# The low part of the FFN's gated tiles: subtracted by POOL instead of DVE

## The reference

```python
def swiglu(h, w_up, w_down):
    g, u = jnp.split(h @ w_up, 2, axis=-1)
    return (jax.nn.silu(g) * u) @ w_down
...
x = x + mix
x = x + swiglu(rmsnorm(x, norm_ffn[layer]), ffn_w_up[layer], ffn_w_down[layer])
```

## Time and profile before

| | us |
|---|---|
| median of 3 runs | 2603.36 |
| lowest and highest | 2598.88 and 2606.93 |
| the profiled execution's own time | 2599.3 |
| its span, first to last instruction | 2597.3 |

### The profile page before, as it was taken

How to read it: one execution, slowest core, us unless ns; L and a number is a source line. 1 busy time by engine, 2 the same in 40 slices (tenths; PEclk the granted TensorE clock), 3 DMA queues, 4 the chain that set the end, 5 groups by cost and what they waited for, 6 DMA issues and landing times.

```text
span 2597.3 us, 36699 instructions
## 1 busy us (share of the span) xinstructions
PE 2480.4 (95%) x15562; PEld 2217.9 (85%) x15562; DVE 1056.5 (41%) x1691; ACT 903.6 (35%) x1182; POOL 1266.8 (49%) x674
## 2 busy tenths in 40 slices
PE   7999998899999999999989899999978999999997
PEld 5889986688787888999979889988866779999997
DVE  3523245344335521544664451154475345222224
ACT  4332344342223412433444241344444223222222
POOL 5645454645545744533534474344342536544554
PEclk9999998999999999999989999999998999999999
DMA  4222233123232232222212222222222223222222
GB/s 161 90 79 73 74 124 102 62 77 110 90 105 81 92 97 97 74 82 82 90 49 90 74 92 94 93 90 73 86 74 96 84 98 122 90 90 91 88 90 82
DMA packets 72322, 233.17 MB, mean 90 GB/s; under 512 B 8768, under 2 KB 10848, under 8 KB 72160
## 3 DMA queue, kind: packets, MB, share of 16 engines
q1 hardware_dynamic: 72160, 230.82, 26.9%
HBM read 221.74 MB, written 9.05 MB: 89 GB/s over the span
## 4 chain that ended last, share of the span: by engine, by line
PE 80%; DVE 7%; ACT 3%; issue 3%; POOLq 2%; POOL 2%; DVEq 1%; DMA 1%; SPq 0%; ACTq 0%
PE ps L670 56%; PE ps L700 17%; POOLq L1172 2%; DMA wr<-in_wblk 1%; DVE xc L1682 1%; POOL wl L1166 1%; ACT wh L954 1%; DVE mixl L1508 1%; PE ps L759 1%; PE ps L757 1%; PE ps L763 1%; DVE sq L1315 1%; DVE vm L1705 0%; DVEq L1522 0%; POOL rsB L1178 0%
## 5 line engine op out<-in xcount | busy, mean ns | idle before, releaser
L1166 POOL TENSOR_TENSOR wl<-wr,wh 128x1024 fp32r<-128x1024 f32 (+2 forms) x396 | 950.6, 2411 | 619.9 <-ACT wh L954 619.1
L670 PE MATMUL ps<-xh,wh 128*128 128x260 f32 (+3 forms) x3312 | 896.5, 325 | 26.4 <-DVE xl L1328 14.8
L670 PE MATMUL ps<-xh,wl 128*128 128x260 f32 (+3 forms) x3312 | 881.7, 321 | 0.0
L670 PE MATMUL ps<-xl,wh 128*128 128x260 f32 (+3 forms) x3312 | 881.6, 321 | 0.0
L670 PEld LDWEIGHTS ps<-xh,wh 128*128 128x128 f32 (+1 forms) x3312 | 550.7, 189 | 90.8 <-issue 44.5
L670 PEld LDWEIGHTS ps<-xh,wl 128*128 128x128 f32 (+1 forms) x3312 | 549.3, 188 | 48.0 <-issue 2.0
L670 PEld LDWEIGHTS ps<-xl,wh 128*128 128x128 f32 (+1 forms) x3312 | 549.5, 189 | 45.7 <-issue 1.9
L954 ACT ACTIVATE wh<-wr 128x1024 fp32r<-128x1024 f32 (+2 forms) x396 | 409.5, 1044 | 481.7 <-DMA wr<-in_wblk 478.0
L700 PE MATMUL ps<-hidh,wh 128*128 128x260 f32 (+1 forms) x1056 | 289.4, 328 | 34.9 <-DVE hf L1529 13.5
L700 PE MATMUL ps<-hidl,wh 128*128 128x260 f32 (+1 forms) x1056 | 285.7, 325 | 0.0
L700 PE MATMUL ps<-hidh,wl 128*128 128x260 f32 (+1 forms) x1056 | 284.7, 324 | 0.0
(11 more groups left out here) (326 smaller groups left out, 2219.2 us busy)
## 6 DMA issues: line engine op xcount, KB each, us to landing
wr<-in_wblk SPq DMA_DIRECT2D x392, 512.0 KB, 3.7
xr<-in_xT SPq DMA_DIRECT2D x8, 260.0 KB, 5.8
xB<-in_xT SPq DMA_DIRECT2D x8, 260.0 KB, 4.5
out_yT<-xB SPq DMA_DIRECT2D x8, 260.0 KB, 2.2
xr<-in_xT SPq DMA_DIRECT2D x8, 256.0 KB, 5.8
xA<-in_xT SPq DMA_DIRECT2D x8, 256.0 KB, 4.3
Ss<-in_s_even SPq DMA_DIRECT2D x1, 2048.0 KB, 9.9
out_ss_even<-Ss SPq DMA_DIRECT2D x1, 2048.0 KB, 9.3
```

Source lines behind the costliest of these rows:

```text
L670: mm = pe.matmul(ps[0:cols, b + c, 0:n], wt[:, w], xt[:, e:e + n], start=first, stop=end)
L1166: pool.tensor_tensor(wl[n % 4][:, 0:w], wr[n % 4][:, 0:w], wh[n % 4][:, 0:w].bitcast(F32), ALU.subtract).then_inc(s_lo, 1)
```

## The change

`hidden_lo` is moved, word for word but for the engine, from DVE's block to POOL's, and the branch `hl` with it. The item's place in the list, its wait on `s_hh` (ACT's `hidh`) and its signal `s_hl` stay.

```diff
@@ POOL's block
+            def hidden_lo(L, X, g, k):
+                pool.wait_ge(s_hh, FI[L, X] * NF + 2 * g + k + 1)
+                t = slice((2 * (g % 2) + k) * W[X], (2 * (g % 2) + k + 1) * W[X])
+                pool.tensor_tensor(hidl[:, t], hf[:, t], hidh[:, t].bitcast(F32), ALU.subtract).then_inc(s_hl, 1)
...
+                elif k == "hl":
+                    hidden_lo(*v)
@@ DVE's block
-            def hidden_lo(L, X, g, k):
-                v.wait_ge(s_hh, FI[L, X] * NF + 2 * g + k + 1)
-                t = slice((2 * (g % 2) + k) * W[X], (2 * (g % 2) + k + 1) * W[X])
-                v.tensor_tensor(hidl[:, t], hf[:, t], hidh[:, t].bitcast(F32), ALU.subtract).then_inc(s_hl, 1)
...
-                elif k == "hl":
-                    hidden_lo(*z)
```

## The result

The changed kernel takes 2604.95 us (median of 21 runs, 2601.73 to 2606.66), the kernel before 2599.06 us (median of 21 runs, 2591.39 to 2606.93). The ratio, taken over all runs, is 1.0025, with a 95% interval of 1.0019 to 1.0032 (the two medians alone give 1.0023): some 6 us slower, where "no change" at 2603 us was forecast. The three runs that the forecast started from had a median of 2603.36 us, 4.3 us above that of all 21. So a time of 2605 us looked like no change against them and is a loss. One execution of 8591.87 us, in the kernel with six tiles taken back, is left out of its ratio.

A forecast was written before the change was run, and what follows sets the result against it. PE, busy 95% of the span, was taken to bound the kernel. Terms 0 + 0 - 3.0 + 0.5 + 1.6 + 0.6 = -0.3 us gave 2599.0, and with the runs' median 4.1 us higher, 2603 us; range 2593 to 2613.

The forecast's parts named there:

- The price of the instruction: One tile's subtraction on POOL: 1.3 us, bounds 1.2 and 2.4; 88 of them add 114 us to POOL.
- Ordinary groups and the wait for `hidl`: FFN groups, and PE's need of the low part: POOL's queue still delivers in time, 0 us each.
- The mixer's splits: Three places in groups 9 and 10: DVE's second split waits less for POOL; -3.0 us, bounds -4.5 to +1.5.
- The rows: Two places at the mLSTM's rows: POOL's run gets longer, PE waits; +1.6 us in all, bounds -1.4 to +2.6.
- The start of layer 0 A: Start of that FFN, where PE waits for POOL's products: +0.6 us, bounds -0.7 and +1.3.
- The RG-LRU: Two places in layer 0 B, one in 1 A: longer POOL runs hold DVE; +0.5 us, bounds -2.4 to +3.9.
- The clock "makes no case": Around the RG-LRU, shifted gaps change lower-clock time; 5 us more or less would be 2.5 us, only widening each case.
- The starting point: Whole kernel: the median of the runs shown, 4.1 us above the profiled execution's 2599.3 us, sets the forecast's level.
- The first rival: Nine places where DVE and POOL meet: longer POOL runs hold DVE the full 1.3 us; 2613 us, chance 0.12.

The follow-up runs named there:

- the kernel with six tiles taken back: Changed kernel, but DVE subtracts the six tiles in groups 6 to 8 of layer 1 A: ratio 0.9997 to the kernel before.
- the kernel with the tile moved: Changed kernel, but POOL subtracts the second tile of layer 1 A's group 6 behind its next gate, about 20 us later: ratio 1.0017 to the kernel before.

## Why the prediction was wrong, point by point

- **The price of the instruction: right.** 1338 ns against 1.3 us, 88 times.
- **Ordinary groups and the wait for `hidl`: right.** Layer 1 B alone gives 0.9998, and PE names no `hidl` in its waits.
- **The mixer's splits: right.** Forecast -1.0 us each, -3.0; in the trace the first gap shrinks by 0.94, the other two by 1.05 each (2.00 to 0.95, 1.74 to 0.69), of which the gap behind the second took 0.28 back (1.42 to 1.70): -2.8 in all. By themselves they gave a ratio of 0.9985, -3.9 us with an interval of -6.5 to -1.6.
- **The rows: near.** Forecast +0.8 each; +0.77 and, in layer 1 A, +0.43 (1.16 to 1.59): +1.2.
- **The start of layer 0 A: near in size, by another path.** Forecast +0.6, from the second subtraction, with the first one's delay covered. It was not covered: the later rotary product made a new gap of 1.46 us at 438.60, while the wait for Q grew by 0.09. From PE's first wait of this FFN to the end of the wait for Q, 0.76 us were left (49.43 in place of 48.67). Layer 0 A alone was 1.0000.
- **The RG-LRU: the step that failed.** The text said "three places with a first subtraction in the chain to a PE gap", took +0.5 us in all and gave POOL "a pause" at the third. (The 5.39 us that it names as a gate and two blocks are the two blocks alone.) Two things were wrong with it. The third place, group 6 of layer 1 A, has no pause for the samples' small instructions: the first subtraction adds 1.0 us to DVE's chain. And only first subtractions were looked at. The second one was left where DVE had done it, between two additions, though POOL takes it as soon as it can, in mid-chain: another 1.0 us. So the term is +0.6 in layer 0 B and +2.0 in layer 1 A: +2.6 where +0.5 was taken, inside its own bounds of -2.4 and +3.9.
- **The clock "makes no case": wrong, as far as is known.** With the terms as measured the sum is -2.8 + 1.2 + 0.8 + 2.6 = +1.8 us, and some 6 were measured. What else moved is the clock: the mean granted clock fell from 0.9761 to 0.9739 over 21 and 11 runs on one chip. If all of that fell where PE was busy it would be 0.0022 x 2600 = 5.7 us; this is a ceiling. The forecast had the size of such a term, 2.5 us for 5 us of the lower level, but let it fall either way. It fell one way, though not by one tile alone: the mean clock was 0.9738 to 0.9754 in the seven sets of runs with the second tile of that group on POOL in mid-chain, and 0.9758 to 0.9765 in eight of the others; but it was 0.9746 with that tile back on DVE and 0.9751 with six back, at ratios of 1.0003 and 0.9997, and 0.9740 with it moved. Where the clock's fall lies was not located: behind the last gap of group 6 the traces show none. So the larger part of the loss is put down to the clock by its mean alone, and its cause stays open.
- **The starting point.** The 2603.36 us of three runs stood 4.3 us high; the forecast added its sum of -0.3 to it. The profiled execution's 2599.3 us was the better guide to 2599.06. That the result lies within 2 us of the forecast 2603 is luck: an error of the start hid the loss. And the 0.3% that the forecast held to be about the limit of what can be told from no change was too wide: over 21 runs the interval reaches 0.0007 to either side, 2 us.

The first rival, slower by the ports, had the right engine and kind of loss, but it priced nine places at 1.3 us and let the splits' gain fail. The splits gained; the rows and the start lost 2.0 us, and one place lost as much by itself.

One tile taken back changes the ratio from 1.0025 or 1.0021 to 1.0003: that this tile decides whether the change loses is shown. Put on POOL alone it costs 1.0009, about half of that, so its effect depends on what else moves. With it back among the 88, the stretch of group 6 was 3.0 us shorter in its one trace (39.2 against 42.3 and 42.2), 1.0 of it in DVE's chain and the rest behind it; but the kernel with the tile moved lacked that second part, and the mean clock rose by only 0.0007. That the two tiles together make DVE's chain 2.0 us longer is shown in fifteen traces. By what way the rest of the loss comes, some 4 us in the changed kernel, was not shown.

## What to carry to other kernels

When a step moves to an engine that runs ahead of the others, ask when that engine will do it, not where it stands in the list: the same item can move in time from behind a critical chain into it. Look at every instance of the step in the stretches where another engine already waits, small instructions of the neighbour included; one tile of 88 decided this change. And put the step where it cuts a long POOL run into pieces: three tiles gave 2 to 4 us, 59 more nothing that can be measured, and with the other 26 the gain became a loss.

## What the hardware showed unexpectedly

Even a DVE instruction on 128x8 or 128x32, 0.2 us by itself, can wait the full 1.3 us for a POOL instruction on 128x512 (1.34 and 1.31 us in the changed kernel). In two executions, time at TensorE's lower level ahead of a wait for another engine was free, and time at it behind the wait cost 2.5 us, with the same instructions and the same DVE chain (clock 0.66 and 1.00 against 0.80 and 0.67). The place of the lower level at the samples in layer 0 A (granted clock 1.00 or 0.80) differed between executions with the same instructions up to there, so a difference of clock between two single traces is no evidence for a change.
